# A decoder step on one core: weight sums, tile work and attention pieces put at other places in each engine's order

## The chip, the core and the metric

The kernel runs on one core of one Trainium2 chip. The metric is the device time of one execution in microseconds (us). Times of a kernel are given as the median over its timed runs; profiles show one execution each. PE is the matrix engine (PEld its weight loads), DVE the vector engine, ACT the scalar (activation) engine, POOL the general one and SP the engine whose queue starts the weight transfers. Each works through its own list of instructions in order; they meet only at semaphores.

## The reference

One inference step of a two-layer decoder, for 512 prompt tokens with 16 meta tokens ahead of them and 8 sequences of 4 sampled tokens, all at width 2048. Layer 0 is gated linear attention (GLA); then one K/V projection; then layer 1, sliding-window attention with 8 groups of 4 query heads, each followed by a gate and an output projection.

```python
def gla_layer(x, s0, norm_w, w_in, w_gk2, b_gk2, onorm, w_out, chunk):
    proj = rmsnorm(x, norm_w) @ w_in
    ...
    o, S = gla_recurrence(q, k, v, g, s0, chunk)
    o = rmsnorm(o, onorm).reshape(B, L, GLA_VAL_DIM) * jax.nn.silu(gate)
    return x + o @ w_out, S

def shared_kv(x, norm_kv, w_kv):
    kv = rmsnorm(x, norm_kv) @ w_kv
...
def swa_layer(x, k, v, norm_w, w_in, sinks, w_out, attend):
    h = rmsnorm(x, norm_w)
    q, gate = jnp.split(h @ w_in, [Q_WIDTH], axis=-1)
    o = attend(q.reshape(B, L, N_Q_HEADS, HEAD_DIM), k, v, sinks).reshape(B, L, Q_WIDTH)
    return x + (o * jax.nn.silu(gate)) @ w_out
```

The weights are fp32. All projections together are by far the most work.

## The kernel before

**Units.** A projection is cut into units: 128 output columns for all tokens, 16 k-blocks deep. To reach fp32 accuracy with fp16 matmuls both operands are split into a high and a low fp16 part, and a k-block is six matmuls (three products, two halves of the tokens); so a unit is 96 matmuls into one of two PSUM buffers `PP[0]` and `PP[1]`, in turn (`project`, L579). Before a unit can start, its 1 MB of weights goes through a chain: transfer (SP, L427); ACT squares and sums them (`unit_sum`, L1126); PE adds that over the partitions with one tiny matmul (`block_sum`, L508), which also waits until the PSUM buffer that it writes in has been emptied; DVE makes a power-of-two scale of it (`unit_scale`, L1617 to L1656); ACT writes the high half (`unit_high`, L1137, two instructions) and DVE the low half (`unit_low`, L1664, two). The tiny matmul of the next unit stands at k-block 4 of the present one.

**Pairs.** Where the activations of a stage are only just being made, `pair` (L606) runs the first two units of the stage side by side, the second three k-blocks behind the first, so that each new activation tile is used twice: at the start of the GLA heads, of the K/V projection, and of the output projection. It holds the tiny matmul of the third unit ahead of its step s = 4. Tile k is made by DVE and ACT (`x_high`, L1153 or L1163; `x_low`, L1669 or L1689), and PE waits for it by `h_ready`.

**The K/V stage.** After the pair, units 2 to 7 run alone. In the same stretch DVE and ACT make the 16 normed tiles that layer 1 reads, in a loop over j = 0 to 7, two tiles (`normed`, L2103, then `x_low`, L1669) in each j, before unit j is moved out of PSUM (`kv_keep`, L1441 and L1442 on ACT, L2122 and L2123 on DVE).

**The group steps.** Layer 1 is a loop over the 8 groups (`group_step`): seven passes of one body and a last one with a body of its own. A step has eight slots, and four units of projection run through them, half a unit in each slot (in the last step two units over six slots). Between the pieces PE does the attention of five batches k, each in four stages, one slot apart: `batch_scores(k)` in slot k (L966, for the last one L973), DVE takes the maximum (`batch_max`, L2170 to L2183), ACT the exponential (`batch_exp`, L1503), DVE the division (`batch_norm`), PE transposes it in slot k + 1 (`batch_pt`, L481), DVE masks it (`batch_keep`, L2213 and L2214), PE multiplies by V in slot k + 2 (`batch_pv`, L1009, the last one L1012 and L1015), and DVE puts it aside or multiplies it into the gate in slot k + 3 (`batch_stash` L2222, `batch_late` L2228, `batch_gate` L2235). Units 0 and 1 of a step are gates: ACT reads them out twice (`gate`, L1198 and L1199) and DVE joins the two (L1724). Before, a slot of PE is

```python
piece(n, 0)
if n < NB:
    batch_scores(i, n)
piece(n, 1)
if 2 <= n < NB + 2:
    batch_pv(i, n - 2)
if 1 <= n < NB + 1:
    batch_pt(i, n - 1)
```

with pieces of four k-blocks each. On ACT an odd slot of the loop is `batch_comb` (L1491), `batch_exp`, `group_sum` (the weights' sum) and then `group_gate` or the read-out of q.

**After the groups** ACT sums the squares of the gated output (L1532), PE adds it over the partitions (L1081), DVE makes the scale and starts the tiles of the output stage, which begins with a pair. At the very end PE sums the squares of the residual rows (L1093) for the last norm.

## Time and profile before

| | |
|---|---|
| timed runs, us | 1952.03, 1953.99, 1955.07: median 1953.99 |
| profiled execution, us | 1960.25, of which its span 1958.7 |
| PE busy in the span | 93% |
| DVE, ACT, POOL busy | 59%, 45%, 10% |

The profiled execution took 6.26 us more than the median of the timed runs. All times of the trace are counted from the start of its span. PE is the engine that is busy nearly throughout, so time is to be looked for in PE's waits and in the work that PE does.

### The profile page before, as it was taken

The page shows a single profiled execution, that of the slowest core. Times are in us where ns is not written, and L with a number is a line of the kernel's source. Part 1 is how long each engine was busy: PE and PEld are TensorE (multiplying, and loading weights), DVE is VectorE, ACT ScalarE, POOL GpSimd, SP SyncE. Part 2 cuts the span into 40 slices and gives each one's busy share as a digit, 9 for nine tenths or more (in the row PEclk, how much of TensorE's full clock was granted, in tenths as well). Part 3 has the DMA queues.
Part 4 walks back from the last instruction along what each step waited for, and adds up shares of the span by engine and source line. Part 5 has one row for each costly group of instructions (what it writes and reads, how often), then busy time and mean ns, then how long its engine had stood idle before and what let it go on. Part 6 is the DMA issues. An engine that isn't in the chain of part 4 may idle for free.

```text
span 1958.7 us, 38118 instructions
## 1 busy us (share of the span) xinstructions
PE 1815.7 (93%) x14695; PEld 1432.7 (73%) x14695; DVE 1147.6 (59%) x2612; ACT 875.7 (45%) x1320; POOL 198.3 (10%) x288
## 2 busy tenths in 40 slices
PE   4999999999999998989998789999999999979995
PEld 3778876677767875777776567777777777758884
DVE  6534647474757556674966775455655565674442
ACT  6544522453244432453244554444545445454442
POOL 2000001010011001100012300210001100001110
PEclk7999999999999998999999899999999999989997
DMA  9233213452155215451254623322222312324432
GB/s 331 71 83 88 57 45 109 126 149 67 55 151 154 66 45 151 139 184 46 75 167 139 202 81 93 89 76 77 62 75 75 96 51 67 92 67 117 121 93 92
DMA packets 269522, 201.82 MB, mean 103 GB/s; under 512 B 7780, under 2 KB 253808, under 8 KB 268096
## 3 DMA queue, kind: packets, MB, share of 16 engines
q1 hardware_dynamic: 251200, 131.69, 24.8%
q0 software_dynamic: 18192, 68.31, 10.1%
q8 instruction: 92, 1.51, 0.3%
q14 instruction: 38, 0.31, 0.1%
HBM read 166.00 MB, written 37.22 MB: 104 GB/s over the span
## 4 chain that ended last, share of the span: by engine, by line
PE 68%; DVE 14%; issue 7%; ACT 7%; DMA 2%; POOL 1%; DVEq 0%; ACTq 0%; POOLq 0%; SPq 0%
PE PP L579 45%; PE PP L831 6%; PE PP L606 3%; PE BS L669 2%; DVE W L1664 2%; ACT AR L1503 2%; PE B L778 1%; ACT wjunk L1126 1%; ACT W L1137 1%; PE BS L729 1%; PE B L700 1%; PE BS L481 1%; DMA W<-in_w_out_a 1%; DVE AR L2170 1%; DVE AR L2181 1%
## 5 line engine op out<-in xcount | busy, mean ns | idle before, releaser
L579 PE MATMUL PP<-H,W 128*128 128x280 f16 (+1 forms) x7488 | 936.6, 285 | 7.8 <-DVE step L1617 4.0
L579 PEld LDWEIGHTS PP<-H,W 128*128 128x128 f16 x7488 | 730.7, 99 | 192.0 <-issue 28.5
L1137 ACT ACTIVATE W<-W,SCL 128x1024 f16<-128x1024 f32 x240 | 262.5, 1139 | 383.7 <-DVE SCL L1620 366.6
L1664 DVE SCALAR_TENSOR_TENSOR W<-W,SCL 128x1024 f16<-128x1024 f32 x240 | 305.0, 1281 | 114.0 <-ACT W L1137 111.9
L1126 ACT ACTIVATE wjunk<-W 128x2048 bf16<-128x2048 f32 x120 | 227.7, 1898 | 26.7 <-DMA W<-in_w_in_a 9.7
L579 PE MATMUL PP<-O,W 128*128 128x272 f16 (+1 forms) x1920 | 230.9, 282 | 0.9 <-DVE AR L2123 0.5
L579 PEld LDWEIGHTS PP<-O,W 128*128 128x128 f16 x1920 | 187.6, 98 | 38.7 <-DVE W L1664 0.7
L831 PE MATMUL PP<-O,W 128*128 128x280 f16 x1536 | 195.6, 289 | 9.8 <-DVE O L1669 5.4
L831 PEld LDWEIGHTS PP<-O,W 128*128 128x128 f16 x1536 | 150.7, 100 | 55.9 <-issue 19.6
L1503 ACT ACTIVATE AR<-AR 128x128 f32<-128x128 f32 x136 | 53.0, 390 | 152.9 <-DVE AR L2183 152.9
L1724 DVE SCALAR_TENSOR_TENSOR O<-AR,O 128x544 f32 (+3 forms) x32 | 23.4, 730 | 86.8 <-ACT AR L1199 86.7
L1889 DVE SCALAR_TENSOR_TENSOR AR<-AR,B 128x512 f32<-128x512 f32 x64 | 44.9, 743 | 43.9 <-PE B L778 43.9
L1617 DVE TENSOR_SCALAR step<-PP 128x1 f32<-128x1 f32 x107 | 16.6, 155 | 89.2 <-PE PP L508 85.0
L1921 DVE SCALAR_TENSOR_TENSOR H<-PP,SCL,H 128x560 f32<-128x560 f32 x48 | 38.4, 799 | 47.9 <-PE PP L831 47.7
L606 PE MATMUL PP<-O,W 128*128 128x280 f16 (+1 forms) x384 | 49.8, 295 | 14.0 <-DVE O L1669 14.0
L1272 ACT COPY AR<-BS 128x512 f32<-128x512 f32 (+1 forms) x20 | 10.6, 530 | 113.4 <-PE BS L729 90.4
L669 PE MATMUL BS<-AR 128*128 128x64 f32 (+1 forms) x512 | 61.3, 272 | 0.0
L669 PEld LDWEIGHTS BS<-AR 128*128 128x128 f32 x512 | 59.9, 192 | 0.7
L1840 DVE SCALAR_TENSOR_TENSOR AR<-AR,B 128x512 f32<-128x512 f32 x32 | 23.7, 747 | 59.2 <-PE B L700 49.4
L606 PEld LDWEIGHTS PP<-O,W 128*128 128x128 f16 x384 | 38.7, 102 | 24.7 <-issue 13.5
L2342 DVE SCALAR_TENSOR_TENSOR AR<-PP,SCL,AR 128x544 f32<-128x544 f32 x16 | 12.5, 784 | 63.5 <-PE PP L579 60.7
L2390 POOL DMA_DIRECT2D out<-AR x32 | 23.4, 732 | 260.2 <-DVE AR L1889 259.9
(318 smaller groups left out, 2050.1 us busy)
## 6 DMA issues: line engine op xcount, KB each, us to landing
W<-in_w_in_a SPq DMA_DIRECT2D x48, 1024.0 KB, 6.0
W<-in_w_in_b SPq DMA_DIRECT2D x32, 1024.0 KB, 6.0
out<-AR POOLq DMA_DIRECT2D x36, 512.0 KB, 4.0
AR<-in_state_gla POOLq DMA_DIRECT2D x32, 512.0 KB, 5.8
W<-in_w_out_b SPq DMA_DIRECT2D x16, 1024.0 KB, 5.8
W<-in_w_out_a SPq DMA_DIRECT2D x16, 512.0 KB, 5.3
W<-in_w_out_a SPq DMA_DIRECT2D x32, 256.0 KB, 3.8
W<-in_w_kv SPq DMA_DIRECT2D x8, 1024.0 KB, 5.7
```

Of the source, the lines that this page charges most:

```text
L579: last = mm(PP[j % 2][:, c, 0:cols], w[:, k, :], x[:, c * cols:(c + 1) * cols], start=s_, stop=e)
L606: last = mm(PP[j][:, c, 0:cols], w[:, k, :], x[:, c * cols:(c + 1) * cols], start=s_, stop=e)
L669: last = mm(bank[:, t * w:(t + 1) * w], a[:, kt, COLS[t]], queries(kt, COLS[t]), start=(kt == 0), stop=(kt == KT - 1))
L831: last = mm(PP[n % 2][:, c, 0:HALF], w[:, blk, :], x[:, c * HALF:(c + 1) * HALF], start=s_, stop=e)
L1126: A(wjunk, x, ACT.Square, accum_out=WSUM[:, j % 2:j % 2 + 1]).then_inc(w_summed, 1)
L1137: A(w_parts(j % 2)[0][:, ks], W[:, j % 2, ks], ACT.Copy, scale=SCL[:, j % 4, 0:1]).then_inc(w_hi, 1)
L1503: A(Pp[:, b, r * P:(r + 1) * P], Cc[:, b, r * P:(r + 1) * P], ACT.Exp, scale=HD ** -0.5, bias=sm[:, b, 4 + r:5 + r], accum_out=sm[:, b, 16 ...
L1664: STT(out=low[:, ks], in0=W[:, j % 2, ks], scalar=SCL[:, j % 4, 0:1], in1=high[:, ks], op0=ALU.mult, op1=ALU.subtract).then_inc(w_ready, 1)
L1724: STT(out=o[:, 0:cols], in0=th[:, j % 2, 0:cols], scalar=1.0, in1=o[:, 0:cols], op0=ALU.add, op1=ALU.mult).then_inc(gate_done, 1)
L1840: STT(out=S[:, kt, :], in0=S[:, kt, :], scalar=el[:, kt, t:t + 1], in1=bank[:], op0=ALU.mult, op1=ALU.add).then_inc(s_ready, 1)
L1889: STT(out=x, in0=x, scalar=el[:, kt, NT + s:NT + s + 1], in1=bank[:], op0=ALU.mult, op1=ALU.add).then_inc(smp_new, 1)
L1921: STT(out=halves(H[:, n, :]), in0=PV(n), scalar=unscale(m), in1=halves(H[:, n, :]), op0=ALU.mult, op1=ALU.add).then_inc(pp_free[n % 2], 1)
```

## The change

Nothing is computed differently; instructions change places, and one sum is taken in two parts.

1. In the three pairs the tiny matmul of the third unit moves from ahead of step 4 to ahead of step 10 (heads), 8 (K/V) and 8 (output). In the GLA output projection that of unit 1 moves from block 2 to block 6 of unit 0.
2. The tiles for layer 1 in the K/V stage are made in shares of 0, 0, 3, 3, 3, 3, 2, 2 in place of 2 in each j.
3. A slot of PE in the group steps has three pieces (3, 3 and 2 k-blocks in the loop) with the scores after the first, the product with V after the second, and the transposes after the third.
4. ACT's sum of weights in slots 1 and 3 of the loop stands ahead of that slot's `batch_comb` and `batch_exp`.
5. In the last group the sum of squares is taken in two parts, prompt columns and sampled columns.
6. The first low half of output unit 1 moves from the end of the last group behind the first tile of the output stage.
7. The last 30 matmuls run by operand in place of by tile.

```diff
+def tiles_b(j):
+    a = (0, 0, 0, 3, 6, 9, 12, 14, 16)
+    return range(a[j], a[j + 1])
...
-            def pair(at_fn, base, half, src, fresh, total, cols=HALF):
+            def pair(at_fn, base, half, src, fresh, total, cols=HALF, total_step=4):
...
-                    if s == 4:
+                    if s == total_step:
                         block_sum(at_fn(*base, 2)[0], 2, total)
...
-                sum_at = 6 if m >= 11 else 2
+                sum_at = 6 if m >= 11 or m == 0 else 2
...
                 def piece(n, h):
                     if not last:
-                        a = NK // 2 * (n % 2) + NK // 4 * h
-                        group_piece(i, n // 2, a, a + NK // 4)
+                        a = NK // 2 * (n % 2)
+                        group_piece(i, n // 2, a + (0, 3, 6)[h], a + (3, 6, 8)[h])
                     elif n < 6:
-                        a = (0, 3, 6, 9, 12, 14, 16)[2 * (n % 3) + h:][:2]
+                        a = (0, 2, 4, 6, 8, 10, 12, 13, 15, 16)[3 * (n % 3) + h:][:2]
                         group_piece(i, n // 3, *a)
...
                     if 2 <= n < NB + 2:
                         batch_pv(i, n - 2)
+                    piece(n, 2)
                     if 1 <= n < NB + 1:
                         batch_pt(i, n - 1)
```

In the K/V stage ACT and DVE walk over other shares of tiles (ACT shown, DVE the same):

```diff
-                for n in (2 * j, 2 * j + 1):
+                for n in tiles_b(j):
                     x_high(H, xs[:, n % 4, :], n, X_B)
```

In the group step of ACT, the moved sum and the sum of squares in two parts:

```diff
                 for n in range(8):
+                    if n % 2 and not last:
+                        group_sum(i, n // 2 + 2)
                     if n < NB:
                         batch_comb(i, n)
                         batch_exp(i, n)
...
-                            group_sum(i, n // 2 + 2)
...
+                if last:
+                    squares(slice(0, SEQ), KV, (NT + GRP) * i + NT)
+                    act.wait_ge(o_summed, i + 1)
+                    squares(slice(SEQ, LIVE), i, (NT + GRP) * (i + 1))
```

On DVE, the low half that goes to the output stage:

```diff
                     if last and n == 7:
                         unit_scale(out_unit_at(0, 1), 1, 2)
-                        unit_low(out_unit_at(0, 1), 1, (0,))
...
-                if n == 5:
-                    unit_low(out_unit_at(0, 1), 1, (1,))
+                if n in (1, 5):
+                    unit_low(out_unit_at(0, 1), 1, (n // 5,))
```

PE in the loop body, from slot 2's first piece on, before: the four transposes or products with V are one row each (L481, L1009), L966 are scores, L508 is the tiny matmul of a unit, and 24 matmuls of L579 are four k-blocks.

```order
616 L579 MATMUL PP<-H,W 128x272 x24
617 L957 REGISTER_ALU
618 L966 MATMUL BS<-AR 128x256 x4
619 L503 REGISTER_ALU
620 L505 REGISTER_ALU
621 L508 MATMUL PP<-WSUM,ones 128x1
622 L579 MATMUL PP<-H,W 128x272 x24
623 L1009 MATMUL B<-AR 64x256 x4
624 L481 MATMUL B<-CST,AR 128x128 x4
```

The same slot after; its lines are numbered L585 (blocks), L972 (scores), L514 (tiny matmul), L1015 (product with V) and L487 (transposes).

```order
617 L585 MATMUL PP<-H,W 128x272 x18
618 L963 REGISTER_ALU
619 L972 MATMUL BS<-AR 128x256 x4
620 L585 MATMUL PP<-H,W 128x272 x6
621 L509 REGISTER_ALU
622 L511 REGISTER_ALU
623 L514 MATMUL PP<-WSUM,ones 128x1
624 L585 MATMUL PP<-H,W 128x272 x12
625 L1015 MATMUL B<-AR 64x256 x4
626 L585 MATMUL PP<-H,W 128x272 x12
627 L487 MATMUL B<-CST,AR 128x128 x4
```

The tiny matmul keeps the same work ahead of it (a slot's transposes, four blocks, the scores); the product with V now comes two blocks behind it in place of four, and two blocks stand between it and the transposes.

ACT in slot 1 of the loop body, before: L1491 and L1503 are the copy and the exponential of batch 1, L1126 the sum of a unit's weights, L1198 and L1199 the read-out of the gate unit.

```order
442 L1491 COPY AR<-BS 128x512
443 L1498 REGISTER_ALU
444 L1503 ACTIVATE AR<-AR 128x128 x4
445 L1505 ACTIVATE AR<-AR 128x4
446 L1119 ISA
447 L1126 ACTIVATE wjunk,WSUM<-W 128x2048
448 L1195 REGISTER_ALU
449 L1197 REGISTER_ALU
450 L1198 ISA
451 L1198 ACTIVATE O<-PP,SCL 128x544
452 L1199 ACTIVATE AR<-PP,SCL 128x544
```

After, the same slot, with L1135 the sum, L1500 and L1512 copy and exponential, L1207 and L1208 the gate:

```order
440 L1128 ISA
441 L1135 ACTIVATE wjunk,WSUM<-W 128x2048
442 L1493 REGISTER_ALU
443 L1500 COPY AR<-BS 128x512
444 L1507 REGISTER_ALU
445 L1512 ACTIVATE AR<-AR 128x128 x4
446 L1514 ACTIVATE AR<-AR 128x4
447 L1204 REGISTER_ALU
448 L1206 REGISTER_ALU
449 L1207 ISA
450 L1207 ACTIVATE O<-PP,SCL 128x544
451 L1208 ACTIVATE AR<-PP,SCL 128x544
```

The sum no longer stands between the exponential and the gate.

DVE in the K/V stage, before, from the end of unit 1's read-out (L2122, L2123): four tiles (L2103, L1669) stand ahead of the scale of unit 3 (L1617 to L1656).

```order
1393 L2122 TENSOR_SCALAR AR<-PP,SCL 64x560
1394 L2123 TENSOR_SCALAR AR<-PP,SCL 64x560
1395 L2103 SCALAR_TENSOR_TENSOR AR<-H,GV,RB 128x560 x2
1396 L1669 TENSOR_TENSOR H<-AR,H 128x560 x2
1397 L2103 SCALAR_TENSOR_TENSOR AR<-H,GV,RB 128x560 x2
1398 L1669 TENSOR_TENSOR H<-AR,H 128x560 x2
1399 L1617 TENSOR_SCALAR step<-PP 128x1
```

After (L2142 and L2143 the read-out, L1637 to L1676 the scale, L1684 the low halves, L2123 and L1689 the tiles):

```order
1393 L2142 TENSOR_SCALAR AR<-PP,SCL 64x560
1394 L2143 TENSOR_SCALAR AR<-PP,SCL 64x560
1395 L1637 TENSOR_SCALAR step<-PP 128x1
...
1400 L1676 TENSOR_SCALAR SCL<-undo,step 128x3
1401 L1684 SCALAR_TENSOR_TENSOR W<-W,SCL 128x1024 x2
1402 L2123 SCALAR_TENSOR_TENSOR AR<-H,GV,RB 128x560 x3
1403 L1689 TENSOR_TENSOR H<-AR,H 128x560 x3
1404 L2142 TENSOR_SCALAR AR<-PP,SCL 64x560
```

The scale and the low halves of unit 3 come straight behind the read-out of unit 1, and three tiles stand ahead of the read-out of unit 2 in place of two.

## Rows read from the trace of the kernel before

**Rows 1.** The page: engines busy, time, share of the span, instructions

```profile
PE 1815.7 (93%) x14695; PEld 1432.7 (73%) x14695; DVE 1147.6 (59%) x2612; ACT 875.7 (45%) x1320; POOL 198.3 (10%) x288
```

**Rows 2.** Busy time by windows, one per pass of the loop; PEclk after POOL

```profile
1311.30:1374.70 63.40, 59.24 (x510) 46.88 (x509) 37.03 (x98) 31.13 (x70) 5.19 (x9) 1.00 0.26 74
1374.70:1438.60 63.90, 60.84 (x510) 47.63 (x508) 37.10 (x98) 31.15 (x70) 5.18 (x9) 0.97 0.27 74
...
sum 445.60, PE 419.65 PEld 330.46 DVE 259.28 ACT 218.26 POOL 35.37; mean PE 59.95 PEld 47.21 DVE 37.04 ACT 31.18 POOL 5.05
```

**Rows 3.** Timeline of PE, one pass: start, duration, what, [idle before, releaser]

```profile
1325.58 0.16 PE L508 MATMUL PP<-WSUM,ones 128*128 128x1 bf16 x1 [0.47 <-ACT AR L1199]
1325.60 2.94 PE L579 MATMUL PP<-H,W 128*128 128x272 f16 x24
1328.85 1.08 PE L1009 MATMUL B<-AR 128*64 128x256 f32 x8 [0.30 <-DVE AR L2214]
...
1344.87 0.16 PE L508 MATMUL PP<-WSUM,ones 128*128 128x1 bf16 x1 [2.24 <-ACT AR L1199]
...
1348.94 1.08 PE L1009 MATMUL B<-AR 128*64 128x256 f32 x8 [1.11 <-DVE O L2235]
...
1350.45 5.72 PE L579 MATMUL PP<-H,W 128*128 128x272 f16 x48
```

**Rows 4.** Timeline of ACT, the same pass, slots 1 and 3

```profile
1322.24 1.89 ACT L1126 ACTIVATE wjunk<-W 128x2048 bf16<-128x2048 f32 x1
...
1335.23 0.56 ACT L1491 COPY AR<-BS 128x512 f32<-128x512 f32 x1
1339.93 0.40 ACT L1503 ACTIVATE AR<-AR 128x128 f32<-128x128 f32 x1 [4.14 <-DVE AR L2183]
...
1341.58 1.89 ACT L1126 ACTIVATE wjunk<-W 128x2048 bf16<-128x2048 f32 x1
...
1344.07 0.70 ACT L1199 ACTIVATE AR<-PP,SCL 128x544 f32<-128x544 f32 x1
```

**Rows 5.** Timeline of DVE, the same pass, from the gate on

```profile
1345.01 0.73 DVE L1724 SCALAR_TENSOR_TENSOR O<-AR,O 128x544 f32 x1 [5.11 <-ACT AR L1199]
...
1348.38 0.42 DVE L2235 SCALAR_TENSOR_TENSOR O<-B,O 128x256 f32 x1
```

**Rows 6.** Timeline of PE in the next pass, the same place

```profile
1408.33 4.61 PE L579 MATMUL PP<-H,W 128*128 128x272 f16 x24
```

**Rows 7.** Timelines at the first pair: PE, ACT, DVE; then a window

```profile
50.78 0.16 PE L508 MATMUL B<-WSUM,ones 128*128 128x1 bf16 x1 [8.61 <-ACT wjunk L1126]
50.80 21.05 PE L606 MATMUL PP<-H,W 128*128 128x280 f16 x162
...
48.63 1.91 ACT L1126 ACTIVATE wjunk<-W 128x2048 bf16<-128x2048 f32 x1 [5.33 <-DMA W<-in_w_in_a]
...
51.32 0.80 DVE L1689 SCALAR_TENSOR_TENSOR H<-AR,GV,H 128x560 f16<-128x560 f32 x1 [4.89 <-ACT H L1163]
...
53.00:56.00 3.00, 3.00 (x23) 2.25 (x22) 3.00 (x5) 1.79 (x3) 0.00 (x0) 0.82 0.00 0
```

**Rows 8.** Timelines in the K/V stage: PE, then DVE

```profile
1157.67 0.16 PE L508 MATMUL PP<-WSUM,ones 128*128 128x1 bf16 x1 [3.36 <-issue]
...
1142.01 1.51 DVE L2103 SCALAR_TENSOR_TENSOR AR<-H,GV,RB 128x560 f32<-128x560 f32 x2
...
1147.93 0.16 DVE L1617 TENSOR_SCALAR step<-PP 128x1 f32<-128x1 f32 x1
...
1170.76 0.80 DVE L2122 TENSOR_SCALAR AR<-PP,SCL 64x560 f32<-64x560 f32 x1 [5.49 <-ACT AR L1442]
```

**Rows 9.** Timelines from the last group to the output pair: PE, then ACT

```profile
1730.82 0.66 PE L1012 MATMUL B<-AR 32*64 32x128 f32 x2 [2.71 <-DVE O L2235]
...
1743.01 5.62 PE L606 MATMUL PP<-O,W 128*128 128x272 f16 x30 [3.88 <-DVE O L1669]
...
1737.04 1.09 ACT L1532 ACTIVATE wjunk<-O 128x1088 bf16<-128x1088 f32 x1
```

More of the change, by code:

```diff
@@ L200, in yoco_kernel @@
         GS = sb("GS", [P, 3])
-        OS = sb("OS", [P, KV])
+        OS = sb("OS", [P, KV + 1])
         out_fix = sb("out_fix", [P, 4])
@@ L850, in head_step @@
                     elif n == 0:
-                        pair(head_unit_at, (0,), 0, H, 0, B3[:, 300:301])
+                        pair(head_unit_at, (0,), 0, H, 0, B3[:, 300:301], total_step=10)
                     if first(h) and n in (3, 5, 7):
@@ L920, in _ @@
                 if j == 0:
-                    pair(lambda n: kv_unit_at(n), (), KVP // 2, O, X_KV, B2[:, 300:301])
+                    pair(kv_unit_at, (), KVP // 2, O, X_KV, B2[:, 300:301], total_step=8)
                 elif j > 1:
@@ L1071, in out_tiles @@
                     if first(i) and j == 0:
-                        pair(out_unit_at, (0,), OUT_B // 2, O, X_OUT, B3[:, 300:301], HALF_B)
+                        pair(out_unit_at, (0,), OUT_B // 2, O, X_OUT, B3[:, 300:301], HALF_B, total_step=8)
                     elif not first(i) or j > 1:
@@ L1087, in _ @@
             pe.wait_ge(acc_done, 2 * NK - 4)
-            pe.wait_ge(sq_a, 2 * NK)
             pe.wait_ge(y_kept, 2 * NK - 2)
-            for t in range(NT + 1):
-                n = LIVE_WID[t]
-                for q, x in enumerate((acc[:], sqa[:, 0, :], sqa[:, 1, :])):
-                    last = mm(B0[0:n, 2 * t:2 * t + 2], x[:, LIVE_COLS[t]], ones[:, 0:2], start=(q == 0), stop=(q == 2))
+            for q, x in enumerate((acc[:], sqa[:, 0, :], sqa[:, 1, :])):
+                if q:
+                    pe.wait_ge(sq_a, 2 * NK - 2 + q)
+                for t in range(NT + 1):
+                    n = LIVE_WID[t]
+                    last = mm(B0[0:n, 2 * t:2 * t + 2], x[:, LIVE_COLS[t]], ones[:, 0:2], start=(q == 0 and t == 0), stop=(q == 2),
+                              skip_group_check=True)
             last.then_inc(ms_done, 1)
@@ L1528, in group_step, with squares @@
                         unit_high(out_unit_at(0, 1), 1)
-                act.wait_ge(b_gated, (NT + GRP) * (i + 1))
-                act.wait_ge(w_summed, U_SWA + 4 * i + 8 if not last else U_OUT + 2)
-                o = O[:, ds(2 * i, 2), 0:LIVE]
-                A(wjunk[:, 0:2 * LIVE].rearrange("p (a n) -> p a n", a=2), o, ACT.Square,
-                  accum_out=OS[:, ds(i, 1)]).then_inc(o_summed, 1)
-                act.wait_ge(o_summed, i + 1)
+                def squares(cols, at, gated):
+                    act.wait_ge(b_gated, gated)
+                    x = O[:, ds(2 * i, 2), cols]
+                    n = cols.stop - cols.start
+                    A(wjunk[:, 0:2 * n].rearrange("p (a n) -> p a n", a=2), x, ACT.Square,
+                      accum_out=OS[:, ds(at, 1)]).then_inc(o_summed, 1)
+                act.wait_ge(w_summed, U_SWA + 4 * i + 8 if not last else U_OUT + 2)
+                if last:
+                    squares(slice(0, SEQ), KV, (NT + GRP) * i + NT)
+                    act.wait_ge(o_summed, i + 1)
+                    squares(slice(SEQ, LIVE), i, (NT + GRP) * (i + 1))
+                else:
+                    squares(slice(0, LIVE), i, (NT + GRP) * (i + 1))
+                    act.wait_ge(o_summed, i + 1)
             for j in (2, 3):
@@ L2133, in _ @@
                     unit_low(kv_unit_at(j + 1), j + 1)
-                for n in (2 * j, 2 * j + 1):
+                for n in tiles_b(j):
                     normed(G_B, n, X_B)
-                for n in (2 * j, 2 * j + 1):
+                for n in tiles_b(j):
                     x_low(H, xs[:, n % 4, :], n, X_B)
@@ L2308, in keep_rows @@
                 V.tensor_copy(YR[0:SMP, NT, ds(n4 * P, P)], b[0:SMP, 0:P]).then_inc(y_kept, 1)
-            dve.wait_ge(o_summed, KV)
+            dve.wait_ge(o_summed, KV + 1)
             V.tensor_reduce(out_fix[:, 0:1], OS[:], AX.X, ALU.add).then_inc(os_ready, 1)
```

## The prediction

> **What bounds the kernel now.** The page comes first: PE is busy for 93% of the span, DVE for 59% and ACT for 45% [rows 1]. None of the edits takes a matmul of any size away, so the change can only give back what PE waits, or add to it. I therefore went through the timeline of PE stage by stage, then at each wait through those of ACT and DVE, to see which chain ended it. Four places matter. In the loop over seven groups a pass takes 63.40 us, 445.60 in all [rows 2], with waits ahead of the tiny matmul L508 (0.47 and 2.24) and of the product L1009 (0.30 and 1.11) [rows 3]. In the first pair PE stands 8.61 at L508 [rows 7]. In the K/V stage it stands 3.36 there [rows 8]. Around the end of the last group it waits 2.71, then 3.88 for the output stage's first tile [rows 9].
>
> The duration shown for a run of matmuls includes a modelled tail: 24 of L579 are shown with 2.94 us, but start to start four k-blocks take 2.79 and eight 5.6, so a k-block is 0.70. By starts the waits are longer than the brackets say: 48 of L579 from 1350.45 would end near 1356.0. I use starts.
>
> **The loop, edits 3 and 4.** ACT's sum of weights takes 1.90 us (1322.24, 1341.58) and stands between the exponential and the gate, whose end (1344.07 + 0.70) releases L508 at 1344.87 [rows 3, 4]. Ahead of the copy it falls into time in which ACT has nothing: in slot 3 ACT is through with the copy at 1335.79 and waits 4.14 for DVE's maximum [rows 4]. There the gate comes the full 1.90 earlier. In slot 1 there is less room: the sum delays the copy of batch 1 by about 1.3, which leaves a gain of 0.6, but scores one block earlier (0.70) move the whole slot forward. The gate of slot 1 ends about 1.5 earlier.
>
> From a gate's end DVE joins the gate, makes a low half and masks the last batch before the product can run: 4.17 us in slot 4 (1344.77 to 1348.94) and 3.4 in slot 2 (1325.4 to 1328.85) [rows 3 to 5]. That chain doesn't change, but PE now comes to the product two blocks after L508 in place of four, 1.4 earlier. So part of the gain turns into a wait there. I walked one pass in the new order, with each duration from this pass and each start at the latest of its engine's last end and its releaser's end. PE's waits by starts are then:
>
> slot 2, L508: 0.54 before, 0 after; product 0: 0.46, then 0.95;
> slot 3, product 1: 0.20, then 0.48;
> slot 4, L508: 2.27, then 0; product 2: 1.26, then 1.62;
> slot 5, product 3: 0.07, then 0.14.
>
> The last one but one: the product was possible at 1348.94; 1.90 of sum and some 1.4 carried over from slot 2 (DVE has almost no pause between) make it 1345.6, and PE gets there near 1344.0. The sum is 4.80 before and 3.19 after. The same walk through the old order gives 63.3 for the 63.40 measured, with two small waits too long, and by the difference of the two walks a pass saves 1.97. So 1.6 to 2.0; a pass near 61.5. Taken alone, the pieces of three without ACT's move would cost 0.5 a pass in the same walk; the move of the sum is what pays.
>
> Three of the seven passes have more: in the pass from 1374.70 the clock is 0.97 in the mean and the first four blocks after the 2.24 wait take 4.61 in place of 2.94 [rows 2, 6]; the clock fell from 2.4 to 1.2 GHz after PE had stood. 1.11 of waiting behind it absorbed most of that, so 0.4 to 0.5 is left in each. With no wait above 1.7 I expect it gone. Seven passes: 445.6 to 7 x 61.5 = 430.5, that is **-15.1** (bounds -10 and -19).
>
> The Trainium skill ("TensorE: Matmul & The Clock Gate", "A second HAM failure mode: psum-queue depth-cycling") says that short idles between groups of matmuls can make the clock swing back and forth and that each fall is paid for. The trace agrees for the wait of 2.24. By that rule more and shorter waits could be worse; it is a rival below.
>
> **The first pair, edit 1.** The sum of unit 2's weights waits 5.33 for its transfer and ends at 50.7; L508 ahead of step 4 waits for it, though steps 4 to 7 have their tiles. Tile 8 ends on DVE at 52.12 [rows 7], since ACT makes it behind that sum. Moved to step 10, PE does steps 4 to 7 in the wait and resumes with step 8 at 52.3, where it used to start step 4 at 50.8 and so reach step 8 near 56.5 at full clock. That is 4.3 us, and 1.7 more for the half clock in which the old restart ran (0.82 from 53 to 56) if it isn't repeated; but PE stands 4 us ahead of step 8, so I take it as repeated. Tile 12, behind DVE's scale of unit 2, now comes just with PE: another 0.1 to 0.5 lost. **-4.2** (bounds -3.2 and -5). Behind the pair everything hangs on PE's end, so it stays.
>
> **The K/V stage, edit 2.** L508 at 1157.67 waited for unit 2's read-out, which stood on ACT and DVE behind unit 3's scale and two tiles; and the scale had started at 1147.93 only because four tiles (from 1142.01) were ahead of it, 5.9 us [rows 8]. With none ahead, the scale starts near 1142.3, the low halves are done at 1146.8, three tiles at 1151.3, and the read-out can follow unit 2's end by its own 3.2 us (ACT's 1.45, then DVE's two of 0.80 as from 1170.76, and the hand-overs). That end is near 1150.9: L508 less its wait is 1154.3, less four blocks 1151.4, less 0.44 that PE stood for the late low halves [rows 8]. L508 then runs at 1154.2. **-3.5** (bounds -2.5 and -3.6). Three tiles in later units fill DVE to about 10 of a unit's 12 us and add no wait. Moving the other L508s gives nothing: in the K/V pair tile 5 and tile 10 bound PE anyway, in the GLA output the wait ahead of block 8 takes up what is saved. Were I wrong there it would be 0.4 and 0.2.
>
> **The last group and the output stage, edits 3, 5, 6.** The same walk for the last group: the tiny matmul of slot 3 goes behind product 1, products come earlier than their masks, and nothing is moved on ACT to pay for it. PE's waits grow by **+1.4**, one of them to 2.9, ahead of product 1. The sum of squares stands on ACT behind the high halves in both orders (1737.04) [rows 9], so its second part is extra: two small instructions, **+0.3**. The low half took no time that counted where it was, as DVE then waited for ACT; behind tile 0 it puts tiles 1 to 4 back by 1.2. PE, at half clock there (30 matmuls in 5.62 us [rows 9]), takes up part: tile 5 is then what it waits for, **+0.8 to +1.5**, say +1.1. L508 at step 8 there saves nothing, it had not waited.
>
> Edit 7 has the same 30 matmuls and the same last one: 0 (at most 0.2).
>
> **Sum:** -15.1 - 4.2 - 3.5 + 1.4 + 0.3 + 1.1 = **-20.0**. The profiled execution (1960.25) would become 1940.2; it was 6.3 above the median, and the median of 1953.99 becomes 1934.
>
> **The rivals.** (a) *The clock falls at the new waits.* Three short waits a pass remain, up to 1.6 us. A fall costs 1.7 (4.61 less 2.94) [rows 6], now with almost no wait behind it to absorb it. Once in every pass: 7 x 1.6 = 11 and no gain of 0.4 x 3, so 1934 + 12 = 1946. For it: the swings seen. Against: four passes took 2.24 without one. Chance 12%. (b) *The loop gives nothing* (the change doesn't do what it says there): the product's chain of 4.17 goes on setting the pace, and PE waits at L1009 for all that it no longer waits at L508. Only pair and K/V gain: 1954 - 7.7 + 2.8 = 1949. The walk speaks against it, since the slot 2 gain reaches slot 4. 6%. (c) *The other side:* two clock falls in each pass, at the products of slots 2 and 4: 2 x 1.7 x 7 = 24, so 1958, slower. It decides from 2.9 us a pass on. The trace has no pass with two falls. 3%. (d) *More:* the first pair keeps its clock, the walk's waits are too long by what they were for the old order (0.3), and the last group absorbs its share: 1929 or less. 9%. The forecast, 1929 to 1940, has 70%.
>
> **The numbers.** The range 1928 to 1944 takes the forecast, most of (d) and the lower part of (a). 0.2% is 3.9 us, about what a measurement of this kernel tells from no change. Faster by that: forecast, (a), (b) and (d), with some doubt in (b), 95%; within: 2%; slower: 3%.
>
> **What would show it.** Passes near 61.5 us; L508 in slots 2 and 4 with no wait from ACT; L1009 in slot 4 with 1.5 or so, from DVE; no block of 24 matmuls of over 3.5 us. The first pair's wait split, some 4 us ahead of step 8 and none at L508. L508 of K/V unit 4 waiting 0.5. The last group 1 to 2 us longer and the output pair's first tiles further apart. The prediction is wrong if the sum on ACT waits for its weights in slot 3 (I see them land only shortly ahead of it), or if clock falls spread.

## The result and the profile after

The changed kernel takes 1945.27 us in the median of 12 runs (1940.22 to 1950.60), the kernel before beside it 1954.00 (12 runs, 1949.40 to 1958.95): a ratio of 0.9956, 95% interval 0.9941 to 0.9972, so 8.6 us faster (5.5 to 11.5). I had said 1934 and 20.0 us less, 1928 to 1944: the sign is right, the size less than half. The profiled execution took 1950.6, its span 1949.0, 9.7 less than the span before. Two executions in a slow state, 9683.82 us of `sum_alone` and 3129.00 us of the kernel before beside it, are left out of every figure given here.

The page's line of busy times answers to [rows 1]: PE works as long as before, 1815.7.

```profile
PE 1815.7 (93%) x14695; PEld 1433.5 (74%) x14695; DVE 1150.0 (59%) x2612; ACT 876.0 (45%) x1322; POOL 197.2 (10%) x288
```

Stage by stage the 9.7 splits as follows (starts of PE in the two traces, rounded; us):

| | forecast | measured |
|---|---|---|
| start of the first pair | 0 | +0.4 |
| first pair | -4.2 | -2.8 |
| between it and the K/V pair | 0 | -0.3 |
| K/V pair and stage, to the loop | -3.5 | -4.7 |
| loop, seven passes | -15.1 | -5.3 |
| last group, with the squares | +1.7 | +1.4 |
| output pair | +1.1 | +1.4 |
| behind it | 0 | +0.3 |

The loop is counted here from the transposes that open a pass, which gives 445.35 before (the windows of [rows 2] begin elsewhere in a pass and give 445.60) and 440.03 after, where I had 430.5. Nearly the whole miss is there. The windows, one per pass (columns as in [rows 2]):

```profile
1235.77:1297.58 61.81, 58.88 (x510) 46.78 (x509) 37.26 (x98) 29.98 (x67) 5.06 (x9) 1.00 0.27 76
1297.58:1361.46 63.88, 60.60 (x510) 47.82 (x509) 37.39 (x98) 31.17 (x69) 5.03 (x9) 0.97 0.27 73
1361.46:1423.67 62.21, 58.93 (x511) 46.79 (x510) 37.44 (x98) 31.18 (x69) 5.04 (x9) 1.00 0.28 77
...
sum 440.03, PE 417.38 PEld 330.26 DVE 261.67 ACT 217.02 POOL 35.37; mean PE 59.63 PEld 47.18 DVE 37.38 ACT 31.00 POOL 5.05
```

Two kinds of pass: four at clock 1.00 (62.21, the first 61.81) and three at 0.97 (63.84 to 63.88). So there are two questions: why a clean pass takes 62.2 and not 61.5 (seven of them 435.1, not 430.5), and why three take 1.66 more (5.0 in all). PE in a clean pass answers to [rows 3]:

```profile
1364.48 0.41 PE L974 MATMUL BS<-AR 64*128 64x16 f32 x4 [0.33 <-issue]
...
1380.27 0.17 PE L514 MATMUL PP<-WSUM,ones 128*128 128x1 bf16 x1
...
1382.67 1.08 PE L1015 MATMUL B<-AR 128*64 128x256 f32 x8 [0.82 <-DVE AR L2234]
...
1397.64 0.17 PE L514 MATMUL PP<-WSUM,ones 128*128 128x1 bf16 x1
1397.67 1.55 PE L585 MATMUL PP<-H,W 128*128 128x272 f16 x12
1401.27 1.08 PE L1015 MATMUL B<-AR 128*64 128x256 f32 x8 [2.05 <-DVE O L2255]
```

The tiny matmuls (L514) of slots 2 and 4 wait for nothing any more, as forecast. By starts PE stands 0.98 at the product of slot 2 (forecast 0.95), 0.24 in slot 3 (0.48), 2.19 in slot 4 (1.62), and 0.49 at the scores of slot 0, where I had nothing. Behind those scores' wait is ACT:

```profile
1362.27 1.10 ACT L1544 ACTIVATE wjunk<-O 128x1088 bf16 x1
1363.27 0.19 ACT L1544 ACTIVATION_READ_ACCUMULATOR wjunk<-O  x1
1363.79 0.59 ACT L1519 COPY AR<-BS 128x512 f32<-128x512 f32 x1 [0.33 <-ACT wjunk L1544]
```

The copy of the cached keys (L1519), which the first scores need, waits until the sum of squares of the pass before is through, and PE now gets there a block earlier (three k-blocks stand ahead of the scores in place of four). Behind the longer wait of slot 4 are DVE and POOL (the timeline of DVE with its low half, L1684, in slots 3 and 4; then that of POOL in the same pass):

```profile
1388.14 1.29 DVE L1684 SCALAR_TENSOR_TENSOR W<-W,SCL 128x1024 f16<-128x1024 f32 x1 [1.50 <-ACT W L1146]
...
1397.59 1.67 DVE L1684 SCALAR_TENSOR_TENSOR W<-W,SCL 128x1024 f16<-128x1024 f32 x1
```

```profile
1397.36 0.83 POOL L2558 COPY AR<-AR 128x560 f32 x1 [33.68 <-PE BS L979]
```

The same instruction takes 1.29 in one slot and 1.67 in the other, where POOL copies the next group's keys beside it. It stands between the gate and the product. In the kernel before, POOL's copy ran and ended while DVE had nothing to do before 1345.01 [rows 5]: the gate came too late to collide with it.

```profile
1342.88 0.65 POOL L2539 COPY AR<-AR 128x560 f32 x1 [34.06 <-PE BS L973]
```

The Trainium skill ("SBUF — State Buffer", "Who interferes with whom") has the rule, that a DVE instruction with two SBUF inputs contends with a GpSimd instruction that reads SBUF; by that rule, the trace agrees (1.67 beside the copy, 1.29 without).

In the pass before it the clock fell at the same wait (compare [rows 6]):

```profile
1337.39 1.08 PE L1015 MATMUL B<-AR 128*64 128x256 f32 x8 [2.04 <-DVE O L2255]
1338.41 2.89 PE L585 MATMUL PP<-H,W 128*128 128x272 f16 x12
1341.09 0.99 PE L487 MATMUL B<-CST,AR 128*128 128x128 f32 x4
```

Twelve matmuls take 2.89 (1.56 in the clean pass) and four transposes 0.99 (0.60), at 1.2 GHz in place of 2.4. By starts the two take 3.51 in place of 1.83, and the pass is 1.66 longer: nothing waits behind them, so it counts in full.

### The profile page after: what moved, and what is told of

Read it like the earlier page. It is cut to its first block, busy times and chain, and to the rows that moved or that the text cites. A ratio compares the mean times of both kernels' runs of the same rounds, so it can differ in the third digit from the quotient of the medians.

```text
span 1949.0 us, 38120 instructions
## 1 busy us (share of the span) xinstructions
PE 1815.7 (93%) x14695; PEld 1433.5 (74%) x14695; DVE 1150.0 (59%) x2612; ACT 876.0 (45%) x1322; POOL 197.2 (10%) x288
## 4 chain that ended last, share of the span: by engine, by line
PE 66%; DVE 14%; ACT 8%; issue 7%; DMA 2%; POOL 1%; DVEq 0%; ACTq 0%; POOLq 0%; SPq 0%
PE PP L585 44%; PE PP L837 6%; PE PP L612 2%; PE BS L675 2%; ACT W L1146 2%; ACT AR L1512 2%; DVE W L1684 2%; PE B L784 1%; ACT wjunk L1135 1%; DVE AR L2190 1%; PE BS L735 1%; PE B L706 1%; DVE AR L2201 1%; PE BS L487 1%; DMA W<-in_w_out_a 1%
## 5 line engine op out<-in xcount | busy, mean ns | idle before, releaser
L585 PE MATMUL PP<-H,W 128*128 128x280 f16 (+1 forms) x7488 | 943.9, 285 | 7.8 <-DVE step L1637 4.0
L585 PEld LDWEIGHTS PP<-H,W 128*128 128x128 f16 x7488 | 727.5, 99 | 206.3 <-issue 43.1
L1684 DVE SCALAR_TENSOR_TENSOR W<-W,SCL 128x1024 f16<-128x1024 f32 x240 | 307.7, 1292 | 108.2 <-ACT W L1146 106.1
L1135 ACT ACTIVATE wjunk<-W 128x2048 bf16<-128x2048 f32 x120 | 227.6, 1897 | 19.4 <-DMA W<-in_w_in_a 9.7
L585 PE MATMUL PP<-O,W 128*128 128x272 f16 (+1 forms) x1920 | 227.9, 280 | 0.5 <-DVE AR L2143 0.5
L585 PEld LDWEIGHTS PP<-O,W 128*128 128x128 f16 x1920 | 186.3, 98 | 36.6 <-issue 0.7
L837 PEld LDWEIGHTS PP<-O,W 128*128 128x128 f16 x1536 | 150.7, 100 | 56.3 <-issue 19.9
L1512 ACT ACTIVATE AR<-AR 128x128 f32<-128x128 f32 x136 | 53.0, 390 | 134.4 <-DVE AR L2203 134.4
L1637 DVE TENSOR_SCALAR step<-PP 128x1 f32<-128x1 f32 x107 | 16.6, 155 | 91.2 <-PE PP L514 87.5
L612 PE MATMUL PP<-O,W 128*128 128x280 f16 (+1 forms) x384 | 50.6, 297 | 15.1 <-DVE O L1689 15.1
L1744 DVE SCALAR_TENSOR_TENSOR O<-AR,O 128x544 f32 (+3 forms) x32 | 23.4, 730 | 61.0 <-ACT AR L1208 60.9
L1015 PE MATMUL B<-AR 128*64 128x256 f32 x256 | 35.8, 399 | 23.7 <-DVE O L2255 14.3
```

Source lines behind the costliest of these rows:

```text
L585: last = mm(PP[j % 2][:, c, 0:cols], w[:, k, :], x[:, c * cols:(c + 1) * cols], start=s_, stop=e)
L612: last = mm(PP[j][:, c, 0:cols], w[:, k, :], x[:, c * cols:(c + 1) * cols], start=s_, stop=e)
L837: last = mm(PP[n % 2][:, c, 0:HALF], w[:, blk, :], x[:, c * HALF:(c + 1) * HALF], start=s_, stop=e)
L1015: last = mm(B3[HD * a:HD * (a + 1), 0:2 * P].rearrange("p (u n) -> p u n", u=2), v, by_half[:, a], start=first_, stop=not first_)
L1135: A(wjunk, x, ACT.Square, accum_out=WSUM[:, j % 2:j % 2 + 1]).then_inc(w_summed, 1)
L1512: A(Pp[:, b, r * P:(r + 1) * P], Cc[:, b, r * P:(r + 1) * P], ACT.Exp, scale=HD ** -0.5, bias=sm[:, b, 4 + r:5 + r], accum_out=sm[:, b, 16 ...
```

## The experiments

Twelve kernels in three groups of four; each group shares its runs of the kernel before. Us are the ratio's, times 1954, over the number of runs given; they can differ by some us from a difference of medians. "Clean" is a pass without a clock fall, and the last three columns are read from one profiled execution of each kernel. The changed kernel has runs only in a set of its own, so a difference between it and a kernel of another group carries the uncertainty of both, 3 to 4 us each. What a part costs or gives is therefore read from the traces.

| kernel | runs | against before, us (95%) | clean pass | passes with a fall | seven passes |
|---|---|---|---|---|---|
| before | | | 63.42 | 3 | 445.4 |
| changed | 12 | -8.6 (-11.5, -5.5) | 62.21 | 3 | 440.0 |
| sum_alone | 5 | -15.6 (-19.9, -11.1) | 61.10 | 0 | 427.7 |
| pieces_alone | 6 | +9.6 (+5.7, +13.3) | 64.40 | 2 | 453.1 |
| tiles_alone | 12 | -1.6 (-4.3, +1.2) | 63.42 | 4 | 445.8 |
| head_alone | 12 | -3.9 (-6.3, -1.6) | 63.42 | 5 | 446.2 |
| tail_back | 6 | -15.8 (-20.1, -11.3) | 62.21 | 3 | 440.0 |
| filled_wait | 6 | -16.6 (-19.9, -13.3) | 62.21 | 0 | 435.1 |
| part_filled | 6 | -18.4 (-22.1, -14.7) | 62.21 | 0 | 435.1 |
| keys_late | 4 | -21.9 (-24.8, -19.0) | 61.82 | 0 | 432.3 |
| copy_first | 6 | -17.4 (-20.5, -14.3) | 61.90 | 2 | 436.6 |
| walk_whole | 6 | -24.0 (-28.7, -19.5) | 61.51 | 0 | 430.6 |
| two_pieces | 4 | -27.2 (-30.3, -24.0) | 61.10 | 0 | 427.7 |
| two_keys_late | 4 | -27.6 (-31.7, -23.4) | 60.84 | 0 | 425.9 |

**One edit at a time.** The kernel before with one edit each. `sum_alone`:

```diff
                 for n in range(8):
+                    if n % 2 and not last:
+                        group_sum(i, n // 2 + 2)
...
-                            group_sum(i, n // 2 + 2)
```

> The kernel before with edit 4 alone: in the loop ACT's sum of weights stands ahead of the copy and the exponential in slots 1 and 3; the pieces stay at four k-blocks. Theory A (the move of the sum is what pays): the tiny matmul in slots 2 and 4 waits under 0.6 us in place of 0.47 and 2.24, the product of slot 4 still waits about 1.1, a pass takes 60.8 by the walk and up to 61.6 if the key copy and POOL's copy cost here what they cost in the changed kernel; seven passes give 12 to 18 us, the median falls by that. Rival B (the product's chain sets the pace, so that the wait only moves from the tiny matmul to the product): a pass of 62.2 or more, 8 us or less.

Theory A. Every pass takes 61.10, and PE in slot 4 is

```profile
1394.07 0.16 PE L508 MATMUL PP<-WSUM,ones 128*128 128x1 bf16 x1 [0.34 <-issue]
1394.10 2.94 PE L579 MATMUL PP<-H,W 128*128 128x272 f16 x24
1398.42 1.08 PE L1009 MATMUL B<-AR 128*64 128x256 f32 x8 [1.38 <-DVE O L2236]
```

with short waits and no fall. One moved line of ACT's list (edit 4) gives 17.7 us in the loop, more than three times what the changed kernel gets there, and -15.6 by the timed runs.

`pieces_alone`:

```diff
-                        a = NK // 2 * (n % 2) + NK // 4 * h
-                        group_piece(i, n // 2, a, a + NK // 4)
+                        a = NK // 2 * (n % 2)
+                        group_piece(i, n // 2, a + (0, 3, 6)[h], a + (3, 6, 8)[h])
...
+                    if not last:
+                        piece(n, 2)
```

> The kernel before with the three pieces of a slot (3, 3 and 2 k-blocks) in the loop alone; the last group and ACT's order stay. Theory A: the pieces cost, since the product comes two blocks behind the tiny matmul in place of four: 63.9 a pass by the walk against 63.4, with a product wait of 2.5 in slot 4, so the median rises by 3.5 us, and by up to 10 more if the clock falls in every pass behind that wait. Rival B: the pieces carry a part of the gain of the changed kernel; the median falls by 3 us or more.

Theory A in sign, and the wait of slot 4 is the 2.5 of the walk; but a clean pass is 1.0 longer than before (the walk said 0.5), and two of seven have a fall on top.

```profile
1366.10:1430.47 64.37, 59.08 (x510) 46.71 (x509) 36.98 (x98) 31.05 (x69) 4.86 (x9) 1.00 0.26 73
1430.47:1496.26 65.79, 60.49 (x510) 47.21 (x509) 36.99 (x98) 31.05 (x69) 4.92 (x9) 0.97 0.26 72
```

`tiles_alone` walks over `tiles_b(j)` on ACT and DVE and changes nothing else; `head_alone` has `total_step=10` in the first pair.

> The kernel before with edit 2 alone (the tiles for layer 1 in shares 0, 0, 3, 3, 3, 3, 2, 2). Theory A: the wait of 3.36 at the tiny matmul of K/V unit 4 becomes 0.4, and the half clock behind it goes too (96 matmuls took 14.4 us there and take 11.6), 6 us in the K/V stage, of which a clock fall ahead of the loop may take 1.7 back: the median falls by 4.5 to 6. Rival B: only the wait is saved, 3.5.

> The kernel before with the tiny matmul of the first pair ahead of step 10 in place of step 4, and nothing else. Theory A: the pair ends 2.8 us earlier against its own start, since the restart at step 8 runs at half clock for longer than the old one at step 4 (24 matmuls in 5.5 us, then 90 in 10.95 where full clock has 10.5): the median falls by 2.4 to 3. Rival B: the 4.2 of the prediction is there and the profiled execution was an unlucky one: 3.8 to 4.5.

For the tiles the timed runs are a miss for both: -1.6, with an interval that reaches to +1.2. The traces show the gain, and in part why it is hard to see. From the start of the K/V pair to the first pass it takes 126.67 with the tiles moved and 131.41 or 131.43 in `sum_alone` and `pieces_alone`, which have them as before (131.36 in the kernel before). But `head_alone`, which has them as before too, takes only 128.57. PE waits there as before, and this time the clock did not fall behind it: the next 96 matmuls took 14.38 in the kernel before and take 11.60 here (the row of before first, then two of `head_alone`).

```profile
1157.70 14.38 PE L579 MATMUL PP<-O,W 128*128 128x280 f16 x96
...
1149.38 0.16 PE L508 MATMUL PP<-WSUM,ones 128*128 128x1 bf16 x1 [3.35 <-issue]
1149.41 11.60 PE L579 MATMUL PP<-O,W 128*128 128x280 f16 x96
```

With the tiles moved a fall comes ahead of the loop in eight traces of ten, and without it the stretch is 125.0 (`tail_back`, `two_keys_late`). So edit 2 gives between 1.9 and 6.4 by where the clock falls, 4.7 in the usual case.

The first pair takes 39.05, 40.88, 40.62 and 40.39 in the four traces with the tiny matmul at step 4 and 35.50 to 36.71 in the ten with it at step 10, 40.2 against 36.1 in the mean: 4.1 us, rival B's number, and the 3.9 of `head_alone`'s timed runs goes with it. The -2.8 of the first comparison had the shortest of the old ones in it. PE there after, to [rows 7]:

```profile
39.55 9.88 PE L612 MATMUL PP<-H,W 128*128 128x280 f16 x60 [0.98 <-DVE H L1709]
52.95 5.70 PE L612 MATMUL PP<-H,W 128*128 128x280 f16 x24 [3.52 <-DVE H L1709]
58.49 0.17 PE L514 MATMUL B<-WSUM,ones 128*128 128x1 bf16 x1
58.52 10.95 PE L612 MATMUL PP<-H,W 128*128 128x280 f16 x90
```

PE does steps 4 to 7 first (60 matmuls with step 3's), waits 3.52 for tile 8, and has no wait at L514; 24 matmuls at half clock and 90 at nearly full clock end the pair.

**Undoing parts of the changed kernel.** `tail_back` undoes edits 5 and 6 and the last group's pieces; `filled_wait` puts spare matmuls where PE waits:

```diff
+                    if n == 4 and not last:
+                        for q in range(20):
+                            mm(PP[0][:, q % 2, 320:512], w_parts(0)[0][:, q % 6, :], parts(H, q % 6)[0][:, 0:192], start=False, stop=False, skip_group_check=True)
                     if 2 <= n < NB + 2:
                         batch_pv(i, n - 2)
```

> The changed kernel with edits 5 and 6 and the last group's pieces undone (the loop's pieces stay). Theory A: the last group is 1.4 shorter, its sum of squares 0.3, the output pair's wait 1.1 to 1.4: the time falls by 2.8 to 3.1 us against the changed kernel. Rival B: what is lost there is given back behind it (the output stage starts its transfers as before and PE hides it), so that the time stays within 1 us.

> The changed kernel with 20 spare matmuls of 192 columns (1.6 us at full clock) ahead of the product of slot 4 in the loop, where PE stands 2.05 to 2.2 us; they write PSUM columns that nobody reads. Nothing else moves. Theory A (the clock falls in the passes because PE stands there): no fall behind it in any pass, all passes 62.2 to 62.3, so the time falls by 1.66 for each pass that fell before, 4 to 7 us against the changed kernel's median, and the spread of the timed runs shrinks. Rival B (the falls have another cause, or the spare matmuls cost more than the wait covers): the passes still show falls, or each takes longer by what spills over, and the time stays or rises.

`tail_back`: from the start of the last group to that of the output pair 54.47 (55.86 changed, 54.48 before), and from there to the last transposes 190.51 (191.69 changed, 190.26 before): 1.4 and 1.2, together 2.6, a little under theory A. Its timed runs are 7 below the changed kernel's against before, more than theory A's 3, though the two intervals leave room for that. The rest is not in the tail: of the 8.6 between the two profiled executions 3.6 lie in the stretch between the first pair and the K/V pair, 1.7 in the clock fall ahead of the loop and 0.8 in the first pair, none of which the edit touches.

`filled_wait`, theory A for the loop (by the timed runs it is 8.0 under the changed kernel, with 4 to 7 expected). PE does 20 spare matmuls and stands 0.39; all seven passes have a clock of 1.00, and the loop is 5.0 shorter with more work in it:

```profile
1289.44:1351.66 62.22, 60.57 (x531) 48.47 (x529) 37.43 (x98) 31.28 (x69) 5.03 (x9) 1.00 0.27 75
...
sum 435.06, PE 423.96 PEld 339.23 DVE 261.71 ACT 217.07 POOL 35.31; mean PE 60.57 PEld 48.46 DVE 37.39 ACT 31.01 POOL 5.04
```

The product still starts when it did, as the clean passes' 62.21 shows. So the falls in the passes do come from PE's standing there. `part_filled` has 5 spare matmuls in place of 20:

> The changed kernel with only 5 spare matmuls (0.4 us) ahead of the product of slot 4, so that PE stands about 1.65 there and the pass is otherwise the same. Theory A (a fall hangs on how long PE stands at a stretch, and 1.65 does not bring it): no falls in the passes, 62.2 each, about as fast as with 20 spare matmuls, 4 to 7 us below the changed kernel. Rival B (the falls ended with POOL's copy moved for another reason, or 0.4 us of work does not help): falls in about three passes of seven, the changed kernel's time.

```profile
1388.55 0.58 PE L1049 MATMUL PP<-H,W 128*128 128x192 f16 x5
1390.76 1.08 PE L1015 MATMUL B<-AR 128*64 128x256 f32 x8 [1.63 <-DVE O L2258]
```

Theory A: a wait of 1.63 or 1.64 in every pass, no fall in seven, and the same 435.06.

**The clean pass.** `keys_late` moves POOL's copy of the keys behind the last product, `copy_first` the key copy of ACT ahead of the squares, `walk_whole` has both:

```diff
-                if again:
-                    pool.wait_ge(sc_done, NB * i)
-                alone(pool)
-                G.tensor_copy(kg, tile(kdup, i)).then_inc(kg_ready, 1)
...
                     pool.wait_ge(pv_done, NB * i)
+                alone(pool)
+                G.tensor_copy(kg, tile(kdup, i)).then_inc(kg_ready, 1)
```

```diff
+                if not last:
+                    key_copy(i + 1)
                 act.wait_ge(w_summed, U_SWA + 4 * i + 8 if not last else U_OUT + 2)
```

> The changed kernel with POOL's copy of the keys (0.83 us, which ran beside DVE's low half in slot 4) moved behind the last product of the group. Theory A (two engines at once slow DVE): that low half takes 1.28 in place of 1.67, the product's wait in slot 4 falls from 2.05 to 1.65, a clean pass takes 61.8 in place of 62.21, and the time falls by 2.8 us, by up to 5 more if the shorter wait ends the clock falls. Rival B: the low half stays at 1.67, no change.

> The changed kernel with ACT's copy of the cached keys moved ahead of its sum of squares at the end of a pass. In the changed kernel PE waits 0.49 at the first scores of a pass for that copy, which stands behind the squares. Theory A (that wait is one of the two parts by which a pass is longer than predicted): it is gone and a clean pass takes 61.7 to 61.9 in place of 62.21, 2 to 3 us in seven; the product's wait of slot 4 stays at 2.05, so clock falls remain in some passes. Rival B (what is gained at the scores is lost again at the product of slot 2): 62.2 as before.

> The changed kernel with both hindrances away that the walk of the prediction had not had: the key copy ahead of the squares, and POOL's copy of the keys behind the last product. Theory A (they are all that separates the walk from the chip): a pass takes 61.3 to 61.5, the 61.36 of the walk, with no clock fall behind a product wait near 1.65, so the loop gives 6 to 7 us against the changed kernel's clean passes and 5 more against passes with falls: about 1934 to 1937, where the prediction had 1934. Rival B: a third hindrance is there and passes stay at 61.8 or more.

`keys_late`, theory A: DVE's low half is back at 1.28, the product waits 1.65 (DVE's timeline, then PE's), a pass takes 61.82 and no clock falls.

```profile
1392.46 1.28 DVE L1684 SCALAR_TENSOR_TENSOR W<-W,SCL 128x1024 f16<-128x1024 f32 x1
```

```profile
1395.76 1.08 PE L1015 MATMUL B<-AR 128*64 128x256 f32 x8 [1.65 <-DVE O L2255]
```

`copy_first`, theory A: 61.90, and with the wait of 2.05 in place two passes fall (63.57 and 63.56). `walk_whole`, theory A: seven passes of 61.50 to 61.52, 430.55 in all; the prediction had 61.5 and 430.5. ACT's timeline at the start of a pass has the copy first:

```profile
1350.41 0.58 ACT L1518 COPY AR<-BS 128x512 f32<-128x512 f32 x1
1350.88 1.12 ACT L1546 ACTIVATE wjunk<-O 128x1088 bf16 x1
```

Its median of 1933.26 is near the 1934 that I had forecast for the changed kernel as it is, but that is in part luck: the kernel before ran at 1956.53 in this group, so the difference is -24.0 where I had -20.0. The loop's term is what it confirms.

**Without the pieces.** `two_pieces` is the changed kernel with pieces of four k-blocks and the tail undone (edits 1, 2, 4 and 7 are left), `two_keys_late` has POOL's copy late as well.

> The changed kernel with the pieces of four k-blocks everywhere and edits 5 and 6 undone: edits 1, 2, 4 and 7 are left. Theory A (the three pieces cost and only the sum's move pays): a pass takes 60.8 to 61.6, the product's wait in slot 4 is about 1.1 to 1.5, clock falls are gone, so the loop saves 4 to 10 us more and the tail 2.8: 7 to 13 us below the changed kernel, near 1933 to 1937. Rival B (the pieces of three do earn something beside the sum's move): it is no faster than the changed kernel with the tail undone.

> Pieces of four k-blocks everywhere, edits 5 and 6 undone, edits 1, 2, 4 and 7 kept, and POOL's copy of the keys behind the last product of the group. Theory A: passes of 60.8 (the walk's number for this order) in place of 61.10, 2 us less than the same kernel with POOL's copy where it was, 1925 to 1928. Rival B: POOL's copy is harmless in this order, no change from that kernel.

Both are theory A for the passes, 61.10 and 60.84 (60.8 in the walk); between the two totals no difference can be told, where 2 us were expected. Against the changed kernel `two_pieces` gives more than its theory A (7 to 13): 12.3 in the loop and 2.6 in the tail by the traces, 18.6 by the timed runs. They are the fastest of all, 0.9861 (0.9845 to 0.9877) and 0.9859 (0.9838 to 0.9880): 1.4% under the kernel before where the change as made has 0.44%.

```profile
1291.51:1352.35 60.84, 59.22 (x511) 46.91 (x510) 37.04 (x98) 31.16 (x69) 4.71 (x9) 1.00 0.28 78
```

## Why the prediction was right and wrong

**The step that failed** is the loop's term, -15.1 where -5.3 was measured, in two of its sentences.

*"Three of the seven passes have more ... With no wait above 1.7 I expect it gone."* The expectation about short waits was right: there is no fall in any pass of the loop with a longest wait of 1.10 to 1.66 (`two_keys_late`, `two_pieces`, `sum_alone`, `part_filled`, `keys_late`, `walk_whole`: 42 passes). Its premise was not: the wait came out at 2.05 (2.19 by starts, where the walk had 1.62), near the 2.24 of before, and three passes fell. Each fall costs 1.66 now, where 0.4 to 0.5 counted before, since no wait is behind it. 5.0 us. This is rival (a), with its price right and three passes in place of seven; that its 1946 is close to the median is owed in part to the next point.

*"The sum is 4.80 before and 3.19 after ... a pass near 61.5."* The walk had each engine's durations from the pass before. Two of them depend on what lies beside or ahead of them, and the change moved just that: the low half beside POOL's copy (0.4), and the key copy behind the squares (0.3 to 0.5). With the two taken away the chip does 61.51. Seven clean passes: 4.6 us.

POOL's copy has a part in both: with nothing but it moved (`keys_late`) the wait of slot 4 is 1.65, no pass has a fall, and the loop gives 13.0 of the 15.1. The prediction's walk does not name POOL, an engine busy for 10%.

**The choice behind it.** I had walked both halves of the loop's change and wrote that the pieces of three alone cost 0.5 a pass and that "the move of the sum is what pays". The signs of both hold; the 0.5 measured 1.0. What the walk did not say is that the two work on each other: with the sum moved, the pieces cost 1.1 a clean pass (62.21 against 61.10), they stretch the wait of slot 4 from 1.38 to 2.05, and the falls come with it. Edit 3 in the loop costs 12.4 us in all (440.0 against 427.7), and takes back most of what edit 4 gives.

**First pair.** -4.2 forecast, -4.1 by the means of the traces; -2.8 in the one comparison. Right, and by its own mechanism: the wait split, with 3.52 ahead of step 8 (some 4 forecast) and half clock behind it.

**K/V stage.** The wait of 3.36 [rows 8] went as worked out (L514 at 1151.38 with 0.41 left). The measured -4.7 lies outside the bounds of -2.5 to -3.6 even so. The term left out that the clock had fallen behind the old wait, 2.8 us, and that it might fall at the hand-over to the loop, 1.7 (24 of L585 in 4.62); that the second takes back part of the first is luck:

```profile
1151.38 0.16 PE L514 MATMUL PP<-WSUM,ones 128*128 128x1 bf16 x1 [0.41 <-issue]
1151.40 11.60 PE L585 MATMUL PP<-O,W 128*128 128x280 f16 x96
...
1211.80 4.62 PE L585 MATMUL PP<-H,W 128*128 128x272 f16 x24 [0.70 <-ACT AR L1471]
```

**Last group and output pair.** +2.8 forecast, +2.6 to +2.8 measured. Of after, to [rows 9]: product 1, with a wait of 2.65 (2.9 in the walk), the product of the last batch, and the output stage's first tiles.

```profile
1700.70 1.98 PE L1015 MATMUL B<-AR 128*64 128x256 f32 x8 [2.65 <-DVE AR L2242]
...
1719.85 0.40 PE L1018 MATMUL B<-AR 32*64 32x128 f32 x2 [3.51 <-DVE O L2255]
...
1731.66 1.52 PE L612 MATMUL PP<-O,W 128*128 128x272 f16 x6 [3.82 <-DVE O L1689]
1733.81 10.46 PE L612 MATMUL PP<-O,W 128*128 128x272 f16 x72 [0.63 <-DVE O L1689]
```

The output pair's number came out, its mechanism only in part: I had PE wait for tile 5, and it waits for the second tile (0.63). The pair also spent longer at half clock: in its first 10 us the granted clock was 0.69 in the mean, 0.80 before. How the 1.4 splits between the two isn't shown.

The K/V pair takes 27.3 before and after, so the move of L514 there gave nothing, as said. For its moves in the GLA output and the output pair, and for edit 7, the traces can't tell: no run has them alone.

By the timed runs the parts seem to add up: -15.6 for the sum's move, +9.6 for the pieces, -1.6 for the tiles, -3.9 for the first pair and the tail's +2.6 (from the traces) are -8.9, and the change as made has -8.6. With the four intervals the sum is uncertain by some 7 us (my estimate from the table), so this proves little. In the traces of the loop the two halves don't add: -17.7 for the sum's move and +7.8 for the pieces would be -9.9, and together they have -5.3.

**What stays open.** The stretch between the first pair and the K/V pair, in which only one tiny matmul moved, takes 1028.8 to 1040.0 us in the fourteen traces, 1040.0 in the one of before and 1039.7 in the one of after. It is the largest part of the spread, and probably part of why kernels of the second and third group are further under the changed kernel by the timed runs than the loop explains (`filled_wait` and `part_filled` 8 to 10 us for 5.0 in the loop, `keys_late` 13 for 7.7, `copy_first` 9 for 3.4). The windows show where most of it goes (before, after, `two_pieces`):

```profile
71.83:1111.82 1039.99, 995.78 (x7866) 775.13 (x7865) 624.08 (x1362) 427.88 (x528) 106.05 (x141) 0.97 0.37 107
69.44:1109.10 1039.66, 995.96 (x7867) 775.51 (x7866) 623.99 (x1362) 427.90 (x528) 105.93 (x141) 0.97 0.37 107
68.65:1097.46 1028.81, 986.41 (x7867) 771.47 (x7865) 624.30 (x1362) 427.88 (x528) 106.04 (x141) 0.98 0.37 108
```

Between the longest and the shortest PE's busy time differs by 9.4 of the 11.2 us, at a lower mean clock: it is mostly clock falls. Why there are more of them in one execution than in another no run here shows.

## What to carry to other kernels

Take a duration into a walk of the new order only after asking what ran beside it and ahead of it on its engine, above all an engine that is busy for 10% only: a chain that moves earlier can move into it. Price each half of a combined change by itself, and if one half has a minus in the walk, say that the change would be faster without it. Look at the longest single wait as well as at the sum of the waits: in this loop a wait of 2.05 us was followed by a clock fall in three passes of seven, at 1.66 each, and one of 1.63 by none, which a few spare matmuls were enough to test.

## What the runs showed that I had not expected

- More work made the kernel faster: 20 spare matmuls a pass, 1.6 us of PE's time, and 5.0 us off the loop.
- Behind the same wait the clock fell in some passes and not in others: of 21 passes with 2.24 (before, `tiles_alone`, `head_alone`) 12 had a fall, of 21 with 2.04 to 2.06 (changed, `tail_back`, `copy_first`) 8, of 7 with 2.50 two, of 49 with 1.66 and less none (the 42 above and `filled_wait`'s seven with 0.83). No run had a longest wait between 1.66 and 2.04. The Trainium skill ("TensorE: Matmul & The Clock Gate", "HAM oscillation — how this bites in real kernels") has its rule for longer idle gaps than these; here the clock fell behind shorter ones.
- Short waits are not safe everywhere, so the longest single wait isn't the whole of it. Ahead of the loop PE stands 1.06 and then 0.70 in all fourteen traces, and in eight of them the clock fell there; all eight have edit 2, two more with it have no fall, and none of the four without it. What decides is not shown.
- The fall is not tied to the program: the wait of 3.35 in the K/V stage had one behind it in three traces and none in `head_alone`.
